# High weights by both activation planes in one product of 512 columns, in nine phases of a two-block transformer kernel

## The reference

```python
# first block
h = rms_norm(x, norm_g)
proj = h @ w_in      # q_a k_a v_a z_a q_i k_i w_i q_b f_b i_b z_b gates
o_a = dsa_attention(rope(norm(q)), rope(norm(k)), v, rope(q_i), ...) 
y_a = o_a * silu(z_a)
y_b = rms_norm(hgrn2_chunkwise(silu(q_b), 1 - f, i_b, log(f))) * silu(z_b)
p = einsum('btnc,ncd->btnd', stack([y_a, y_b]), w_branch)
merged = sum(sigmoid(gates) * p, axis=branch)
x = x + merged @ w_out
# second block
h = modulate(rmsnorm(x, norm1_g), sh1, sc1)
q, k, v, f, hy = split(h @ w_in_2);  kc, vc = split(hc @ w_in_2[...])
y = merge_groups(neighbourhood_attention(q, k, v, kc, vc), fourier_mix(f), hyena_mix(hy, ...))
x = x + g1 * (y @ w_out_2)
gate, up = split(modulate(rmsnorm(x, norm2_g), sh2, sc2) @ ffn_w_up)
x = x + g2 * ((gelu(dwconv_centred(gate)) * up) @ ffn_w_down)
return rmsnorm(x, final_norm_g)
```

## Time and profile before

| | us |
|---|---|
| median of 3 runs | 2232.84 |
| lowest and highest | 2229.89, 2233.9 |
| the profiled execution's own time | 2229.55 |
| its span, first to last instruction | 2227.8 |
| TensorE busy | 2171.2 |
| VectorE busy | 1453.3 |
| ScalarE busy | 1029.0 |

### The profile page before, as it was taken

One profiled execution on the slowest core, in us unless ns is written; L12 is line 12 of the kernel. 1 busy time (PEld: TensorE's weight loads), 2 busy tenths in 40 slices (PEclk: granted clock), 3 DMA queues, 4 the chain that ended last, 5 costly groups with the idle time before them and its releaser, 6 DMA issues.

```text
span 2227.8 us, 37995 instructions
## 1 busy us (share of the span) xinstructions
PE 2171.2 (97%) x16534; PEld 2019.3 (91%) x16534; DVE 1453.3 (65%) x1796; ACT 1029.0 (46%) x1394; POOL 6.3 (0%) x10
## 2 busy tenths in 40 slices
PE   7999999999999999999999999979999999999996
PEld 7989989878999999998888999979999999988885
DVE  7666546556757697696665677776666665555654
ACT  6554334334455555454433454554444443444453
POOL 0000000000000000000000000000000000000000
PEclk9999999999999999999999999989999999999998
DMA  9765655665447978786565756747676675555552
GB/s 320 251 203 195 187 195 175 198 200 175 146 150 260 314 232 268 257 280 220 180 207 157 239 167 210 246 159 236 229 238 235 232 237 190 185 192 194 189 193 91
DMA packets 344261, 469.55 MB, mean 211 GB/s; under 512 B 20446, under 2 KB 318302, under 8 KB 331103
## 3 DMA queue, kind: packets, MB, share of 16 engines
q1 hardware_dynamic: 344094, 467.12, 63.0%
HBM read 465.00 MB, written 2.10 MB: 210 GB/s over the span
## 4 chain that ended last, share of the span: by engine, by line
PE 94%; DVE 4%; ACT 2%; issue 0%; DMA 0%; SPq 0%; DVEq 0%; ACTq 0%
PE ps L1804 67%; PE ps L1811 11%; PE ps L1819 4%; PE ps L1889 1%; PE ps L1831 1%; DVE wlo L1104 1%; ACT whi L561 1%; PE ps L2166 1%; PE ps L2099 1%; PE ps L2093 1%; PE ps L2061 1%; PE ps L1941 1%; PE ps L1958 0%; PE ps L2053 0%; PE ps L1979 0%
## 5 line engine op out<-in xcount | busy, mean ns | idle before, releaser
L1104 DVE TENSOR_TENSOR wlo<-raw,whi 128x1024 fp32r<-128x1024 f32 (+1 forms) x668 | 815.0, 1222 | 721.9 <-ACT whi L561 719.9
L561 ACT ACTIVATE whi<-raw 128x1024 fp32r<-128x1024 f32 (+1 forms) x668 | 705.8, 1057 | 1126.0 <-PE ps L1804 921.0
L1804 PE MATMUL ps<-phi,whi 128*128 128x256 f32 (+2 forms) x3744 | 775.3, 288 | 7.7 <-DVE plo L1561 6.8
L1804 PE MATMUL ps<-plo,whi 128*128 128x256 f32 (+2 forms) x3744 | 744.9, 280 | 0.0
L1804 PE MATMUL ps<-phi,wlo 128*128 128x256 f32 (+2 forms) x3744 | 743.9, 280 | 0.0
L1804 PEld LDWEIGHTS ps<-phi,whi 128*128 128x128 f32 (+1 forms) x3744 | 573.4, 188 | 48.1 <-issue 36.2
L1804 PEld LDWEIGHTS ps<-plo,whi 128*128 128x128 f32 (+1 forms) x3744 | 571.5, 188 | 0.5
L1804 PEld LDWEIGHTS ps<-phi,wlo 128*128 128x128 f32 (+1 forms) x3744 | 571.4, 188 | 0.5
L1170 DVE SCALAR_TENSOR_TENSOR arena<-raw,cst,arena 128x1024 f32<-128x1024 f32 x120 | 153.5, 1280 | 3.5 <-DVE arena L1251 0.5
L1811 PE MATMUL ps<-whi,dhi 128*128 128x512 f32 x352 | 94.1, 389 | 0.0
L1811 PE MATMUL ps<-whi,dlo 128*128 128x512 f32 x352 | 94.1, 389 | 0.0
(11 more groups left out here) (347 smaller groups left out, 2113.2 us busy)
## 6 DMA issues: line engine op xcount, KB each, us to landing
raw<-w_in_dram SPq DMA_DIRECT2D x151, 1024.0 KB, 6.4
raw<-ada_w_dram SPq DMA_DIRECT2D x96, 1024.0 KB, 5.0
raw<-ffn_w_up_dram SPq DMA_DIRECT2D x88, 1024.0 KB, 5.1
raw<-ffn_w_down_dram SPq DMA_DIRECT2D x44, 1024.0 KB, 5.1
raw<-w_out_dram SPq DMA_DIRECT2D x32, 1024.0 KB, 5.6
raw<-w_branch_dram SPq DMA_DIRECT2D x16, 1024.0 KB, 7.0
arena<-xT_dram SPq DMA_DIRECT2D x4, 544.0 KB, 6.4
arena<-ctxT_dram SPq DMA_DIRECT2D x1, 2048.0 KB, 10.6
```

What stands on the lines that cost most here:

```text
L561: nc.scalar.activation(whi[c % 4][:, 0:w], src, ACT.Copy).then_inc(S("split_hi"), 1)
L1104: v.tensor_tensor(wlo[c % 4][:, 0:w], src, whi[c % 4][:, 0:w].bitcast(F32), ALU.subtract).then_inc(S("split_lo"), 1)
L1804: l = mm(ps[2 * p + h][0:m, b:b + tt.stop - tt.start], wx[:, k], x[:, xi, tt], start=first, stop=last)
```

## The change

In the nine phases of PAIRED, the planes phi and plo become halves of one tensor, planes. For each k-tile and output half, one product of 512 columns multiplies the high weights by both planes: the bank's columns 0:256 get high by high, columns 256:512 high by low. The product of the low weights by phi adds into columns 0:256. Each k-tile has four products (and four weight loads) instead of six. The two banks stay in turn; in the unit's last k-tile the low weights come first, and elsewhere the high.

The two halves of a bank must be added. ScalarE's ev_T copies columns 256:512 at the place where it copied the result, and raises low_out; VectorE's new add_high adds columns 0:256 in the slot of the next unit's first chunk and then gives the bank back (gemm_free). In F, resid has four additions instead of two, in the same slot as before. In L both kinds of unit are copied and added that way, the gates to gsum and the others to actT; the convolution is then computed from gsum in the slots of the odd unit (ScalarE in its second slot, VectorE in its third, GELU in its fourth), and the last multiplication follows add_high of the odd unit. ScalarE's wait for the last gates moves from before the E phase to the second slot of E.

```diff
+PAIRED = ("QI", "ZB", "ZA", "GA", "GB", "F", "IF", "IQ", "L")
+LOW_OUT = {}
+for _u, (_n, _k, _i) in enumerate(UNITS):
+    if _n in PAIRED and _n != "F":
+        LOW_OUT[_u] = len(LOW_OUT) + 1
...
-        phi = sb("phi", [128, KT, T], F32R)
-        plo = sb("plo", [128, KT, T], F32R)
+        planes = sb("planes", [128, 2, KT, T], F32R)
+        phi, plo = planes[:, 0], planes[:, 1]
...
-        cgt = R(15360, 2, 256)
+        cgt, gsum = R(15360, 2, 256), R(15872, 2, 256)
...
                 p = u % 2
+                pair = UNITS[u][0] in PAIRED
                 act.wait_ge(S("mm"), C0[u + 1])
                 for h in range(2):
-                    c = nc.scalar.activation(dst[:, n * h:n * h + n], ps[2 * p + h][:, 0:n], ACT.Copy)
-                c.then_inc(S(f"gemm_free{p}"), 1)
+                    c = nc.scalar.activation(dst[:, n * h:n * h + n], ps[2 * p + h][:, 256 * pair:256 * pair + n], ACT.Copy)
+                c.then_inc(S("low_out" if pair else f"gemm_free{p}"), 1)
...
+                elif name == "L":
+                    if i % 2:
+                        ev_T(u, actT[:, 256 * (i - 1):256 * (i - 1) + 512], 256)
+                    else:
+                        ev_T(u, gsum[:, :, :].rearrange("p a b -> p (a b)"), 256)
...
+                if q == 1:
+                    wait_evacs(act, u - 1)
                     for h in range(2):
...
+                        nc.scalar.activation(cgt[:, h, :], gsum[:, h, :], ACT.Identity,
+                                             scale=cols[:, V_FCW1 + i - 1 + h:V_FCW1 + i + h],
+                                             bias=cols[:, V_FCB + i - 1 + h:V_FCB + i + h]).then_inc(S("cv_mid"), 1)
+                if q == 3:
                     act.wait_ge(S("cv_all"), 12 + i + 1)
                     nc.scalar.activation(cgt[:, :, :], cgt[:, :, :], ACT.Gelu_apprx_tanh).then_inc(S("gelu"), 1)
...
-            wait_evacs(act, U0["GB"] + 7)
...
+                    if i == 0:
+                        wait_evacs(act, U0["GB"] + 7)
                     g = gates[:, :, 512 * i:512 * i + 512]
...
-                for h in range(2):
-                    c = x1T[:, 2 * i + h, :]
-                    m = v.tensor_tensor(c, c, ps[2 * p + h][:, 0:256], ALU.add)
+                for half in range(2):
+                    for h in range(2):
+                        c = x1T[:, 2 * i + h, :]
+                        m = v.tensor_tensor(c, c, ps[2 * p + h][:, 256 * half:256 * half + 256], ALU.add)
+                    if half == 0:
+                        chain(m)
                 m.then_inc(S(f"gemm_free{p}"), 1)
...
+            def add_high(u):
...
+                dve.wait_ge(S("low_out"), LOW_OUT[u])
+                for h in range(2):
+                    m = v.tensor_tensor(dst[:, 256 * h:256 * h + 256], dst[:, 256 * h:256 * h + 256], ps[2 * p + h][:, 0:256], ALU.add)
+                if name == "L" and i % 2:
+                    chain(m)
+                    dve.wait_ge(S("gelu"), i // 2 + 1)
+                    m = v.tensor_tensor(dst, dst, cgt[:, :, :].rearrange("p a b -> p (a b)"), ALU.mult)
                 m.then_inc(S(f"gemm_free{p}"), 1)
...
-                    elif name == "L":
-                        glu(u, i)
+                if q == 0 and u - 1 in LOW_OUT:
+                    add_high(u - 1)
+                glu(c)
...
+                        if name in PAIRED:
...
+                            for low in ((True, False) if en else (False, True)):
+                                for h in range(2):
+                                    k = slice(n * k4 + 128 * h, n * k4 + 128 * h + 128)
+                                    if low:
+                                        l = mm(ps[2 * p + h][:, 0:256], wl[:, k], xh[:, kt, cc], start=False, stop=False)
+                                    else:
+                                        l = mm(rx(ps[2 * p + h][:, :], 2), wh[:, k], planes[:, :, kt, cc], start=st, stop=en)
+                            continue
```

More of the change, by code:

```diff
@@ L685, in evacuate, with glu @@
                     ev_N(u, v2, i)
-            def glu_mid(u):
-                p = u % 2
+            def glu(c):
+                u, q = CHUNK[c]
                 i = u - U0["L"]
-                if i % 2 == 0:
-                    act.wait_ge(S("mm"), C0[u + 1])
+                if UNITS[u][0] != "L" or i % 2 == 0:
+                    return
+                if q == 1:
+                    wait_evacs(act, u - 1)
                     for h in range(2):
[L694 to L699, removed]
+                        nc.scalar.activation(cgt[:, h, :], gsum[:, h, :], ACT.Identity,
+                                             scale=cols[:, V_FCW1 + i - 1 + h:V_FCW1 + i + h],
+                                             bias=cols[:, V_FCB + i - 1 + h:V_FCB + i + h]).then_inc(S("cv_mid"), 1)
+                if q == 3:
                     act.wait_ge(S("cv_all"), 12 + i + 1)
@@ L718, in slot @@
                 if c + 1 == C0[u + 1]:
[L719 to L722, removed]
+                    evacuate(u)
+                glu(c)
                 if c in CLOSE_AT:
@@ L1223, in resid2 @@
                     m = v.scalar_tensor_tensor(c, ps[2 * p + h][:, 0:256], modL[:, 16 * G1 + kt:16 * G1 + kt + 1], c, ALU.mult, ALU.add)
+                m.then_inc(S(f"gemm_free{p}"), 1)
+            def add_high(u):
+                name, _, i = UNITS[u]
+                p = u % 2
+                w = 512 * i
+                if name == "QI":
+                    dst = q_i[:, w:w + 512]
+                elif name == "ZB":
+                    dst = z_b[:, w:w + 512]
+                elif name == "ZA":
+                    dst = z_a[:, w:w + 512]
+                elif name == "GA":
+                    dst = gates[:, 0, w:w + 512]
+                elif name == "GB":
+                    dst = gates[:, 1, w:w + 512]
+                elif name == "IF":
+                    dst = fT[:, w:w + 512]
+                elif name == "IQ":
+                    k = 2048 * (i % 2) + 512 * (i // 2)
+                    dst = qkT[:, k:k + 512]
+                elif i % 2:
+                    dst = actT[:, 256 * (i - 1):256 * (i - 1) + 512]
+                else:
+                    dst = gsum[:, :, :].rearrange("p a b -> p (a b)")
+                dve.wait_ge(S("low_out"), LOW_OUT[u])
[5 more added lines that the diff above has]
+                    m = v.tensor_tensor(dst, dst, cgt[:, :, :].rearrange("p a b -> p (a b)"), ALU.mult)
                 m.then_inc(S(f"gemm_free{p}"), 1)
@@ L1240, in convolve, with glu @@
                 dve.sem_inc(S(f"gemm_free{p}"), 1)
-            def glu(u, i):
-                p = u % 2
-                if i % 2 == 0:
+            def glu(c):
+                u, q = CHUNK[c]
+                i = u - U0["L"]
+                if UNITS[u][0] == "L" and i % 2 == 1 and q == 2:
                     for h in range(2):
-                        dve.wait_ge(S("cv_mid"), 12 + i + (h + 1))
-                        v.scalar_tensor_tensor(cgt[:, h, 1:256], ps[2 * p + h][:, 0:255], cols[:, V_FCW0 + i + h:V_FCW0 + i + h + 1],
+                        dve.wait_ge(S("cv_mid"), 12 + i - 1 + (h + 1))
+                        v.scalar_tensor_tensor(cgt[:, h, 1:256], gsum[:, h, 0:255], cols[:, V_FCW0 + i - 1 + h:V_FCW0 + i + h],
                                                cgt[:, h, 1:256], ALU.mult, ALU.add).then_inc(S("cv_left"), 1)
                     for h in range(2):
-                        dve.wait_ge(S("cv_left"), 12 + i + (h + 1))
-                        v.scalar_tensor_tensor(cgt[:, h, 0:255], ps[2 * p + h][:, 1:256], cols[:, V_FCW2 + i + h:V_FCW2 + i + h + 1],
+                        dve.wait_ge(S("cv_left"), 12 + i - 1 + (h + 1))
+                        v.scalar_tensor_tensor(cgt[:, h, 0:255], gsum[:, h, 1:256], cols[:, V_FCW2 + i - 1 + h:V_FCW2 + i + h],
                                                cgt[:, h, 0:255], ALU.mult, ALU.add).then_inc(S("cv_all"), 1)
[L1253 to L1261, removed]
             def slot(c):
```

1 line of the change is left out of this document (added).

## The result

The changed kernel is slower by 0.25%: median 2235.81 us (2234.36 to 2238.96) against 2229.96 us (2227.94 to 2233.9) for the kernel before. The ratio is 1.0025, with a 95% interval of 1.0018 to 1.0033. I had forecast 2209 us, faster, in a range of 2203 to 2221. The profiled execution took 2236.54 us, its span is 2234.8.

What follows compares the result with a forecast made beforehand. TensorE's products were taken as the bound. Fewer products -29.7 us, two stands +5.5 and gain not earned +0.8 gave -23.4 us: 2206.2 on the profiled execution's scale, 2209 us on the median's, range 2203 to 2221.

Steps and rivals of the forecast that it cites:

- What bounds the kernel: Where nine tenths of the changed products run, time is the number of TensorE products times the time of one.
- The price of a two-plane product: Paired phases: a 512-column product over both planes takes 223.7 ns, saving 10.3 ns per pair, 29.7 us in sum.
- The 512-column row: M0 and M1 products at 226.7 ns, taken as upper bound; as a rival saves 21.0 us, 2218 us, chance 0.17.
- the dearer bound: Two-plane product at 226.7 ns instead of 223.7, beside low-weight products of 117.0 ns; saves 7.3 ns per pair.
- The stands: Slots IQ+24 and IQ+32: TensorE's attention products wait for VectorE's additions, 2.1 and 3.4 us, sum +5.5 us.
- The clock stays: The stretches concerned are granted 1.00, and TensorE does not become less busy in them; no cost.
- Nothing gives it back: The 5.5 us of waiting at attention steps 8 and 12 stays lost, since TensorE is the bound again at once.
- The slower one: Rival: the jump between planes costs as much as starting a product, 234.0 ns or more; 2238 us, chance 0.10.
- The rival that only 2.1 ns are paid per product: Only a product's start goes, 6.0 us in all against 5.5 and 0.2; 2232 to 2233 us, chance 0.08.
- the bound in F or L: Rival: VectorE becomes the bound in F, or a hidden chain in QI to GB adds 5 us; 2214, chance 0.07.
- The 0.8 us not earned beside the rotations: In about ten chunks of ZB and ZA, shorter products only lengthen TensorE's wait for VectorE's rotations: 0.8 us.
- The rule of the Trainium skill: Columns / 2.4 + 2.5 ns per warm product: a merged pair saves 2.5 ns, 7.2 us in sum instead of 29.7.

Runs made afterwards that it cites:

- forms B and C: In L's k-tiles 1 to 14, changed kernel with 528-column k-tiles and IQ's additions early: B six products of 256, 117.0 ns each; C only two of 512, 230.9 ns each.
- a16: The changed kernel's four products in L's k-tiles, 512-column k-tiles, planes starting 16 columns past a multiple of 2048 bytes: 690.0 ns per k-tile.
- the control: Kernel before, six products of 256 per k-tile, second block's planes at 512 columns per k-tile starting 16 columns past: 2235.18 us, ratio 1.0018.

## Why the prediction was wrong

**What bounds the kernel: right.** TensorE's products are the time, in the changed kernel too; 60 us more of VectorE's work (1453.3 to 1512.8) cost nothing by itself.

**The price of a two-plane product: wrong, and with it the whole forecast.** I took 223.7 ns between bounds of 223.7 and 226.7; it is 230.9 by itself (some 232 in the mix of L), and the low-weight product beside it went from 117.0 to 119. The step that failed is "The 13.3 is the same at both lengths: it is paid per product (or per weight load, ...), not per column", and what was drawn from it for these planes, "the addition is paid once and is 10.3 ns with these planes: 213.3 + 10.3 = 223.7 ns". It was 17.6 ns at 512 columns. The rows for it, the context planes' 256 columns and M0's 512, both have operands that start at the same place within 256 bytes; there it is true (226.7, 173.4, 120.0). For phi and plo I carried it over with the argument that their products are 3 ns cheaper at 256. They are cheaper at 256 and dearer at 512: with k-tiles of 272 columns the planes stand off from the weights by 64, 128 or 192 bytes in three k-tiles of four, and there a product of 512 took 229 to 233 ns and one of 256 some 118. The prediction had seen the difference in layout and read its sign at one length as valid at the other. The 512-column row was then no upper bound.

Per k-tile I had 681.4 ns (2 x 223.7 + 2 x 117.0) and got 702, so all of the 29.7 us went. Of the 20.6 ns 14.4 are the two long products, 3.6 the two short ones (118.8 by themselves), and 2.6 come from mixing them. The layout alone is not the whole of it: at equal starts the four products take 697 ns and at the best start 690, still more than I forecast and more than the 687.4 of the dearer bound. That merging gained nothing is two things together: in this layout the merged product is dearer (230.9 for 226.7) and the six it replaces are cheaper (117.0 for 120.0).

**The stands: right in place, nearly in size.** 1.85 and 3.18 us of idle time for 2.1 and 3.4; IQ lost 2.1 us as forecast. What was missing is the clock: "The clock stays" held in the stretches that it named, but in OA, after the second stand TensorE ran at 1.2 GHz for 3.4 us, another 1.6 us. "Nothing gives it back" was right, and it cost more than itself. The experiment that moves the additions took back 4.9 of the 5.9 us lost between the medians.

**Rivals.** The slower one, 2238 us with a chance of 0.10, came nearest in time (2235.8) and in its arithmetic: nothing saved, the stands remain. Its mechanism, the jump from plane to plane, is refuted by the unbroken run of 512. The rival that only 2.1 ns are paid per product had the gain nearly right for this layout (3.1 ns for a pair made one, by forms B and C, and none in the mix) and should have had more than 0.08; but I let 226.7 speak against it, a row of another layout. Apart from these, no unit waited for a bank and VectorE did not become the bound in F or L, as said. The 0.8 us not earned beside the rotations could not show, there being nothing to earn.

**The rule of the Trainium skill** ("TensorE: Matmul & The Clock Gate", section "Back-to-back issue gap": columns / 2.4 + 2.5 ns, given there for an isolated product) would have given 7.2 us of gain and, with the stands, no change. No run has that spacing for these products: at equal starts it is 13.3 ns over the columns, and with the changed kernel's starts 17.6 at 512. But its consequence, that little is to be had from fewer products, was nearer than mine.

**What stays open.** Why the distance of the two operands within 256 bytes matters: no run shows the cause. Why four mixed products take more than the sum of the same alone (702 against 461.8 + 237.6 with 528 columns), so that the total came out equal to six of 117.0 to the nanosecond, is open as well. That a16 is the best mix was measured, not explained, and so was the unit at 16 columns that took 228.9 ns. The first block's paired phases were not brought to constant starts; what merging would be worth there was not measured.

## What to carry to other kernels

A price per product and a price per column can't be told apart by one length in one layout; take the row of the same operands at two lengths, or count on both. Before merging products to save their fixed cost, look where weights and moving operand start: here merging was worth nothing with starts that change from k-tile to k-tile, and 11 us (0.5%; 15 us against the control) once every k-tile started 64 bytes past the weights' place. And where a result is finished in a slot later than before, look through the queue of the engine that is the bound for work that reads it in that slot; such a stand costs more than itself if the clock falls after it, here 3.2 us and another 1.6.

## What the runs showed of the hardware

- A float32r product of 256, 384 and 512 columns took 120.0, 173.4 and 226.7 ns with weights and moving operand at equal starts within 256 bytes, and 117.0, 174.7 and 230.9 ns with starts that change by 64 bytes per k-tile. It is the distance that counts: both moved by 64 bytes, 226.7 at 512 columns; one alone by 16 to 192 bytes, 231 to 234 (one unit at 64 bytes: 228.9).
- The mix of two products of 512 and two of 256 was best at a constant distance of 64 bytes: 690.0 ns, against 696.7 at equal starts and 702 at changing ones.
- A moving operand of two runs 17408 bytes apart took the same as one unbroken run of 512 columns.
- 2880 weight loads fewer, with the same columns, changed nothing that could be measured at changing starts (ratio 1.0002, 0.9992 to 1.0011, once the stands were gone).
- A stand of TensorE of 3.18 us was followed by 3.4 us at a granted clock of 0.50, and in three more kernels by at least as much; one of 1.85 us was not. An idle time of 2.91 us was followed by it in three of the eight profiles of whole kernels.
